# One encoder layer on one core: first loads and first norm by blocks of tokens, and a reordered preparation of the pairs of heads

## The reference, cut to what matters

```python
hn = rms_norm(h, norm_mix)
proj = hn @ w_in                      # 2048 x 5248
u_r, q, k, v = split(proj)
u_r = u_r + mu_prev * (prev - u_r) + mu_next * (next - u_r)   # first 3712 columns
y_r = rwkv7_bidirectional(u_r, ...)   # 16 heads of 64: LoRA terms, a state of 64x64 per head and direction
y_a = rms_norm(window_attention(q, k, v, sink, bias))
h = h + concat([y_r, y_a]) @ w_out
h = h + memory_cross_attention(rms_norm(h), rms_norm(mem))
h = h + hierarchical_moe(rms_norm(h))
return rms_norm(h, final_norm)
```

## Time and profile before

| | before |
|---|---|
| median of 3 runs | 1913.31 us (1912.08 to 1913.46) |
| the profiled execution's own time | 1915.28 us |
| its span, first to last instruction | 1913.5 us |
| busy: PE, DVE, ACT, POOL | 88%, 23%, 16%, 4% |
| mean granted TensorE clock | 0.964 |

### The profile page before, as it was taken

The page is one execution under the profiler, slowest core; times in us unless marked ns, Lnnn a source line. Parts: engine busy times, 40 slices in busy tenths (PEclk is TensorE's granted clock), DMA queues, the critical chain, the costliest instruction groups (busy, mean ns, idle before and its releaser), DMA issues.

```text
span 1913.5 us, 36816 instructions
## 1 busy us (share of the span) xinstructions
PE 1676.4 (88%) x16304; PEld 1194.8 (62%) x16304; DVE 447.1 (23%) x1018; ACT 313.7 (16%) x806; POOL 86.0 (4%) x143
## 2 busy tenths in 40 slices
PE   3999999978788899999899798888988889888884
PEld 2888888867667644766777456555565555655552
DVE  1100333477776410112311011110111101111014
ACT  2112222155556300113100000000000000000001
POOL 1000000000000000002000000000000000000000
PEclk9999999999888999999899999999999999999997
DMA  9734333500000274332399999999999999999995
GB/s 312 129 67 156 125 113 131 213 20 3 4 3 4 84 270 176 133 154 95 143 426 421 428 430 418 425 435 418 431 422 426 434 415 430 421 412 433 425 434 240
DMA packets 95221, 509.75 MB, mean 266 GB/s; under 512 B 39308, under 2 KB 43808, under 8 KB 77072
## 3 DMA queue, kind: packets, MB, share of 16 engines
q1 hardware_dynamic: 86376, 487.65, 63.0%
q0 software_dynamic: 7808, 17.28, 2.9%
q10 hardware_dynamic: 936, 3.28, 0.6%
HBM read 497.66 MB, written 23.10 MB: 272 GB/s over the span
## 4 chain that ended last, share of the span: by engine, by line
PE 68%; DMA 20%; DVE 6%; issue 2%; ACT 2%; SPq 1%; DVEq 0%; POOL 0%; ACTq 0%
PE ps L1887 18%; DMA ring<-in_wu 18%; PE ps L1385 14%; PE ps L1710 6%; PE ps L1875 6%; PE ps L1937 6%; PE ps L1728 1%; PE ps L1779 1%; PE ps L1737 1%; SPq L271 1%; PE ps L1796 1%; PE ps L1538 1%; PE ps L1467 1%; PE ps L1426 1%; PE ps L1448 1%
## 5 line engine op out<-in xcount | busy, mean ns | idle before, releaser
L1887 PE MATMUL ps<-ring,rkv 128*64 128x256 f32 x4096 | 469.4, 390 | 69.8 <-DMA ring<-in_wu 46.8
L1887 PEld LDWEIGHTS ps<-ring,rkv 128*64 128x64 f32 x4096 | 333.1, 140 | 214.2 <-DMA ring<-in_wu 56.1
L1385 PE MATMUL ps<-hnT,ring 128*128 128x256 f32 (+1 forms) x1280 | 282.2, 379 | 2.1 <-ACT hnT L468 0.9
L1385 PEld LDWEIGHTS ps<-hnT,ring 128*128 128x128 f32 (+1 forms) x1280 | 239.1, 187 | 47.6 <-issue 10.1
L1937 PE MATMUL ps<-ring,gg 128*64 128x512 f32 x1024 | 236.5, 615 | 32.3 <-DMA ring<-in_wd 16.2
L1937 PEld LDWEIGHTS ps<-ring,gg 128*64 128x64 f32 x1024 | 83.7, 142 | 163.1 <-issue 143.9
L1301 DVE SCALAR_TENSOR_TENSOR gg<-ps,tmp,gg 128x256 f32<-128x256 f32 x32 | 15.5, 484 | 519.7 <-PE ps L1887 519.7
L1875 PE MATMUL ps<-hnT,sw 128*128 (+1 forms) x1024 | 122.7, 282 | 4.5 <-DVE hnT L1236 2.4
L1875 PEld LDWEIGHTS ps<-hnT,sw 128*128 128x128 f32 x1024 | 119.4, 197 | 10.6 <-issue 8.3
L727 ACT ACTIVATE rkv<-ps 128x512 f32<-128x512 f32 x32 | 19.1, 597 | 546.1 <-PE ps L1937 546.1
L1309 DVE COPY rkv<-ps 128x512 f32<-128x512 f32 x31 | 21.4, 692 | 242.7 <-PE ps L1937 242.7
(11 more groups left out here) (340 smaller groups left out, 1627.5 us busy)
## 6 DMA issues: line engine op xcount, KB each, us to landing
ring<-in_wg SPq DMA_DIRECT2D x32, 4096.0 KB, 19.8
ring<-in_wu SPq DMA_DIRECT2D x32, 4096.0 KB, 21.4
ring<-in_wd SPq DMA_DIRECT2D x32, 4096.0 KB, 18.1
ring<-in_w_in SPq DMA_DIRECT2D x7, 4096.0 KB, 15.1
ring<-in_w_out SPq DMA_DIRECT2D x4, 4096.0 KB, 22.5
ring<-in_w_in SPq DMA_DIRECT2D x16, 512.0 KB, 7.5
y_dram<-tmp POOLq DMA_DIRECT2D x1, 4096.0 KB, 21.7
ring<-in_xatt_wk SPq DMA_DIRECT2D x1, 4096.0 KB, 13.9
```

Of the source, the lines that this page charges most:

```text
L1385: ins = mm(ps[0:rows_, m % 2, 0:T], lhs, hnT[:, k, :], start=k == 0, stop=k == KD - 1)
L1887: ins = mm(ps[CAP * h:CAP * h + CAP, bank, 0:T], xT[:, k, CAP * i:CAP * i + CAP], slot_k(slot)[:, k, T * h:T * h + T], start=k == 0, stop= ...
```

## The change

1. `x` comes in two transfers of 128 tokens (`x_in0`, `x_in1`). SP's six parameter rows go out ahead of the weights n=0, and the three LoRA matrices move from ACT's queue to SP's, behind n=1 and ahead of n=2 (and ahead of SP's wait for `prm_tr`).
2. The first norm goes by blocks of 128 tokens: squares, square root, reciprocal, scaling and 16 transposes for one block, then the other. DVE's wait for the turned parameters stands between the blocks. The copies out still need both blocks.
3. ACT loads the square root table with a dummy activation on `warm` right behind its first issues, again at the start of each pair but the last, and the exponential table behind the copies of the solutions.
4. `quotients(p + 2)` moves ahead of DVE's wait for step 7; `products_ar(p + 1, 1)` behind the copy `Yp`.
5. ACT's exponentials 0 to 2 wait for DVE's first carried terms (`rw_tte`) and not for `rw_gnow`; number 3 moves behind the copies of states and keeps the wait for `rw_gnow`.

```diff
-            sp.dma_start(tokA[:], xv).then_inc(S["x_in"], 16)
+            for b in range(TB):
+                sp.dma_start(tokA[:, b], xv[:, b]).then_inc(S[f"x_in{b}"], 16)
+            rows(sp, 1)
...
-                if n == 1:
-                    rows(sp, 1)
                 if n == 2:
+                    sp.dma_start(dw2, ...); sp.dma_start(aw2, ...); sp.dma_start(gw2, ...)
                     sp.wait_ge(S["prm_tr"], 1)
...
             pool (first):
+            pool.memset(warm, 1.0)
...
             rows(act, 0)
-            act.dma_start(dw2, ...); act.dma_start(aw2, ...); act.dma_start(gw2, ...)
+            A(warm, warm, ACT.Sqrt)
...
-            squares(0, S["x_in"], 16)
-            std(0, 1)
+            for b in range(TB):
+                act.wait_ge(S[f"x_in{b}"], 16)
+                A(tokB[:, b, :], tokA[:, b, :], ACT.Square, accum_out=stat(0, 0)[:, b:b + 1]).then_inc(S["sq_done"], 1)
+                act.wait_ge(S["first_var"], b + 1)
+                A(stat(0, 2)[:, b:b + 1], stat(0, 1)[:, b:b + 1], ACT.Sqrt).then_inc(S["first_std"], 1)
...
             def exponential(p, n, now=False):
                 if n == 0:
                     act.wait_ge(S["rw_q"], p + 1)
-                    if not now:
-                        act.wait_ge(S["rw_gnow"], p)
+                if n == 3 and not now:
+                    act.wait_ge(S["rw_gnow"], p)
...
             ACT, pair_:
+                if not last:
+                    A(warm, warm, ACT.Sqrt)
                 for g in range(4):
                     act.wait_ge(S["rw_x0"], 4 * p + g + 1)
...
                 if next_:
-                    for n in range(4):
+                    A(warm, warm, ACT.Exp)
+                    act.wait_ge(S["rw_tte"], 4 * p + 1)
+                    for n in range(3):
                         exponential(p + 2, n)
...
                 if next_:
-                    for n in range(4, 8):
+                    for n in range(3, 8):
                         exponential(p + 2, n)
...
             DVE, first norm:
-            normed(0)
-            dve.wait_ge(S["prm_tr"], 1)
-            V.tensor_copy(prm[:, 0:208], ps[:, 7, 0:208]).then_inc(S["prm_ok"], 1)
+            for b in range(TB):
+                one = slice(b, b + 1)
+                dve.wait_ge(S["sq_done"], b + 1)
+                V.tensor_scalar(stat(0, 1)[:, one], ...).then_inc(S["first_var"], 1)
+                dve.wait_ge(S["first_std"], b + 1)
+                dc.link(V.reciprocal(stat(0, 2)[:, one], stat(0, 2)[:, one]))
+                V.tensor_scalar(tokB[:, b, :], tokA[:, b, :], ...).then_inc(S[("first_hn", "hn_done")[b]], 1)
+                if b == 0:
+                    dve.wait_ge(S["prm_tr"], 1)
+                    V.tensor_copy(prm[:, 0:208], ps[:, 7, 0:208]).then_inc(S["prm_ok"], 1)
...
             DVE, pair_:
+                if next_:
+                    quotients(p + 2)
                 dve.wait_ge(S["rw_pt"], 24 * p + 8)
                 if not first:
                     variance(ps[:, 7, T:2 * T])
                 V.tensor_copy(PRN[0][:, 3]...).then_inc(S["rw_pv"], 1)
-                if next_:
-                    quotients(p + 2)
...
                     V.tensor_copy(gam_now, gam).then_inc(S["rw_gnow"], 1)
-                    products_ar(p + 1, 1)
                 dve.wait_ge(S["rw_y0"], 2 * p + 2)
                 V.tensor_copy(Yp..., ps[:, 0:4, T:T + CH]).then_inc(S["rw_y0e"], 1)
                 if not last:
                     dve.wait_ge(S["rw_gnow"], p + 2)
+                    products_ar(p + 1, 1)
                     products_bk(p + 1, 1)
...
             PE, first turn:
-            pe.wait_ge(S["hn_done"], 1)
-            turn(0)
+            for b in range(TB):
+                pe.wait_ge(S[("first_hn", "hn_done")[b]], 1)
+                for k in range(KD):
+                    ins = tr(ps[:, k // 2, ...], tokB[:, b, P * k:P * k + P], ident)
```

More of the change, by code:

```diff
@@ L129, in encoder @@
         exps = sb("exps", [P, 32])
+        warm = sb("warm", [P, 1])[:]
         ps = ctx.enter_context(nc.psum_tensor("ps", [P, 8, 512], F32))
@@ L283, in _ @@
                     sp.wait_ge(used[s], uses[n] - 1)
-                if n == 1:
-                    rows(sp, 1)
                 if n == 2:
+                    sp.dma_start(dw2, a["decay_w2"].rearrange("z r c -> r z c")).then_inc(S["lora_in"], 16)
+                    sp.dma_start(aw2, a["iclr_a2"].rearrange("z r c -> r z c")).then_inc(S["lora_in"], 16)
+                    sp.dma_start(gw2, a["gate_w2"].rearrange("(k p) c -> p k c", p=P)).then_inc(S["lora_in"], 16)
                     sp.wait_ge(S["prm_tr"], 1)
@@ L567, in _ @@
                         exponential(0, n, now=True)
-                    std(4, 2)
+                    std(4, 1)
                 if j == 21:
@@ L623, in _ @@
             squares(1, S["mem_in"], 16)
-            std(1, 3)
+            std(1, 2)
             turned(1)
             squares(2, S["op_add"], 8)
-            std(2, 4)
+            std(2, 3)
             for f in range(4):
@@ L765, in normed @@
                 dve.wait_ge(S["sq_done"], 2 * n + 2)
-                rstd(n, D, EPS, n + 1 if n == 0 else n + 2)
+                rstd(n, D, EPS, n + 1)
                 for b in range(TB):
@@ L789, in turned @@
                     ins.then_inc(S["hn_ev_v"], 1)
-            normed(0)
-            dve.wait_ge(S["prm_tr"], 1)
-            V.tensor_copy(prm[:, 0:208], ps[:, 7, 0:208]).then_inc(S["prm_ok"], 1)
+            for b in range(TB):
+                one = slice(b, b + 1)
+                dve.wait_ge(S["sq_done"], b + 1)
+                V.tensor_scalar(stat(0, 1)[:, one], stat(0, 0)[:, one], 1.0 / D, EPS, ALU.mult, ALU.add).then_inc(S["first_var"], 1)
+                dve.wait_ge(S["first_std"], b + 1)
+                dc.link(V.reciprocal(stat(0, 2)[:, one], stat(0, 2)[:, one]))
+                V.tensor_scalar(tokB[:, b, :], tokA[:, b, :], stat(0, 2)[:, one], None, ALU.mult).then_inc(S[("first_hn", "hn_done")[b]], 1)
+                if b == 0:
+                    dve.wait_ge(S["prm_tr"], 1)
+                    V.tensor_copy(prm[:, 0:208], ps[:, 7, 0:208]).then_inc(S["prm_ok"], 1)
             dve.wait_ge(S["prm_ok"], 1)
@@ L1064, in _ @@
             dve.wait_ge(S["ya_sq"], 3)
-            rstd(4, C, EPS, 2)
+            rstd(4, C, EPS, 1)
             for b in range(TB):
@@ L1372, in _ @@
             pe.wait_ge(S["prm_ok"], 1)
-            pe.wait_ge(S["hn_done"], 1)
-            turn(0)
+            for b in range(TB):
+                pe.wait_ge(S[("first_hn", "hn_done")[b]], 1)
+                for k in range(KD):
+                    o = T * (k % 2) + P * b
+                    ins = tr(ps[:, k // 2, o:o + P], tokB[:, b, P * k:P * k + P], ident)
+                    if b and k % 2:
+                        ins.then_inc(S["hn_tr"], 1)
             pe.wait_ge(S["hn_ev_a"], 4)
```

15 lines of the change are left out of this document (6 added, 9 removed).

## The result

| | before | after |
|---|---|---|
| median of 4 runs each, same chip | 1912.69 us (1910.31 to 1913.46) | 1867.14 us (1865.04 to 1867.9) |
| the profiled execution's own time | 1915.28 us | 1867.9 us |
| its span | 1913.5 us | 1865.8 us |
| mean granted TensorE clock | 0.964 | 0.974 |

The change is faster: ratio 0.9762, interval 0.9745 to 0.9779. The gain is 45.6 us between the medians and 47.7 between the two spans, where 39.9 were forecast.

A forecast was written before the change was run, and what follows sets the result against it. TensorE carries 68% of the chain, so edits pay where it waits, at the start and in the pairs. 18.0 + 15.75 + 4.15 + 2 = 39.9 us from 1915.28 leaves 1875.4; less 1.97, 1873.4; range 1863 to 1884.

The forecast's parts named there:

- my sum: Whole kernel: the forecast's terms add up as priced, time 1868 to 1879 us; chance 0.58.
- the clock stays up: Rival for the pairs: TensorE's clock stays up in all of them, 8 us more than taken, time 1865; chance 0.09.
- The start, 18.0 forecast: Up to the first projection tile: 18.0 us won, between 18.8 (tokens decide) and 9.2 (n=0 at its old pace).
- So the weights decide: At the start: weights n=0, landing at 20.0, let go the first tile, as tokens would allow it at 19.2.
- Full pairs, 15.75 forecast: Pairs 1 to 5: 3.15 us won a pair through `quotients`, `products_ar` and ACT's earlier loads and exponentials, 15.75 in all.
- signs named ahead: Pairs: DVE idle at most 1.5 us before step 7, reciprocal behind root, L1667 not waiting for ACT, L1050 every 31 us.
- its bound of 3.9 a pair: Full pairs, upper bound: 2.54, 0.85 for ACT, and some 0.5 if TensorE takes the states sooner.
- The clock, 2 forecast: Pairs: shorter TensorE waits may keep the clock up in some, at most 10 us, against 4 lost; 2 us gain taken.
- Pairs 0, 6 and 7, 4.15 forecast: Remaining pairs: 2.2 us net in pair 0, 1.95 in pair 6, nothing in pair 7; together 4.15.
- n=0 at its old pace: Rival at the start: weights n=0 land at 28.8, gain there 9.2 us, time 1882; chance of n=0 late 0.14.
- Pairs at half their gain through another wait: Rival: TensorE's solutions or ACT's copies take over, 1.3 to 1.8 us a pair, time 1882; chance 0.13.
- The low clock moving into the Gram products: Rival, slower: low clock moves into Gram products and 24 steps, 8.7 us a pair, time 1934; chance 0.03.

The follow-up runs named there:

- lora_act: The changed kernel with the three LoRA matrices back on ACT's queue, behind its rows: 1879.86 us, ratio 0.9833.
- rows_back: The changed kernel with SP's six parameter rows back between the weights n=0 and n=1: 1876.14 us, ratio 0.9793.
- no_act: The changed kernel with the exponentials' order and waits as before and no dummy exponential: 1883.33 us, ratio 0.9836.
- better: The changed kernel with less DVE work between step 7 and `Yp`, the last gate product going to POOL: 1864.97 us, ratio 0.9742.
- no_ar: The changed kernel with `products_ar` back ahead of the copy `Yp`: 1873.31 us, ratio 0.9782.
- start_only: The changed kernel with the edits in the pairs undone: 1896.28 us, ratio 0.991.
- fill_before: The kernel before with 14 filler matmuls a pair into parts of PSUM that nothing reads: 1910.59 us, ratio 0.9986.
- no_quot: The changed kernel with `quotients` behind step 7 again: 1886.1 us, ratio 0.9849.
- no_loads: The changed kernel without the two dummy activations in the pairs: 1881.28 us, ratio 0.9832.
- pairs_only: The kernel before with only the pair edits (points 3 to 5), without the dummy root ahead of the first norm: 1884.1 us, ratio 0.9854.
- changed_again: The changed kernel itself once more, on the same chip as better: 1866.23 us, ratio 0.9755.
- no_quot_fill: The kernel no_quot with the 14 filler matmuls a pair of fill_before added: 1893.92 us, ratio 0.9883.

## Why the prediction was right or wrong

**Direction and places of the gains: right.** The start and the pairs both gave, as two sums that add up, and the stages behind passed the gain on. The size came near, but its terms missed both ways: less at the start, more in the pairs' order, the clock and pairs 6 and 7, and 1.1 lost behind the pairs. At 1867.14 the time lies just below the 1868 to 1879 of "my sum", and nearer the 1865 of the rival "the clock stays up", to which the prediction gave 0.09.

**The start, 18.0 forecast, 16.5 measured.** n=0 was sized well: forecast 20.0, landed 20.2, and lora_act and rows_back show both of the reasons given. The step that failed was "So the weights decide". Tokens were forecast ready at 19.2 and were at 21.56, for two reasons. The transposes of block 1 ended at 20.06 (13.80 + 6.26), not 18.3: they began at 13.80 and not at 13.1, and the 32 ran without a gap but took 6.26 us, 0.20 each, and not 5.17. With the same code for the start they took 4.93 us in no_act, 5.06 in better, 5.25 in no_ar and up to 6.46 in start_only, all at a granted clock of 1.00, so this part belongs to the execution; what sets it is open. And behind the last transpose I took 0.92 us from before, where the copies had begun early and had kept pace with the transposes (31.93 to 37.10):

```profile
33.16 0.88 DVE L788 TENSOR_SCALAR hnT<-ps,prm 128x256 f32<-128x256 f32 x2 [1.29 <-PE ps L1365]
```

Each copy needs both blocks; so now all 16, eight on DVE and eight on ACT, lie behind 18.01. They take 3.23 us there without a gap, and the tile follows the last of them. In the three kernels with short transposes the copies began 0.6 to 0.8 us earlier, and the tile came at 20.57 to 20.75: the copies decide, and not the 32 transposes' end.

**Full pairs, 15.75 forecast.** Measured are 25.8 in all, of which the clock is a part. In pair 3 (the rows' "pair 2"), which ran from 498.27 to 532.45 before and from 469.58 to 498.46 after, the gains are, stretch by stretch:

| step | forecast | measured |
|---|---|---|
| to step 7 (Gram products, 24 steps) | 0 | 12.05 to 11.64: 0.41 (clock) |
| step 7 to the reciprocal | 1.86 | 3.99 to 1.92: 2.07 |
| reciprocal to L1033 | 0 | 9.81 to 9.82: 0 |
| L1033 to the copy `Yp` | 0.68 | 2.88 to 2.12: 0.76 |
| `Yp` to the chain of states | 0.61 | 2.04 to 1.06: 0.98 |
| the chain to the end of the pair | 0 | 3.41 to 2.32: 1.09 (clock) |

Without the two rows of the clock, whose work did not change, the order gave 3.81, as fill_before says by another way (3.78). Of the three terms only the last was much mis-sized: I let the chain begin 1.44 us behind `Yp`, and it began at 1.06. In no_quot's pair 5, where the chain waits for nothing either but the clock is low, it began 1.31 behind (572.71 to 574.02); so 0.25 of the 0.38 is the full clock, which counts here only because ACT's wait is gone: in fill_before, at the full clock but with ACT's wait, it is 2.05 as before. Of the signs named ahead, the wait for step 7 (1.12, under 1.5), the reciprocal behind the root and the chain without a wait for ACT came as said; the pair's length, 28.9 and not 31, did not. 3.8 × 5 = 19.0, 3.3 above the forecast and inside its bound of 3.9 a pair.

The remark on ACT's table loads held: the dummy activation starts 1.30 us after its load (470.39 to 471.69), and ACT stands for nothing more. The Trainium skill, ScalarE: Activation LUTs, section What ACT_TABLE_LOAD costs, adds 1.38 us of drain to each switch. By it, one switch back on the path costs 2.66 us. no_loads puts one back, the root's, and lost 1.42 at the full clock, with the activation 1.29 us behind the start of its load (552.69 to 553.98). The measurement decides, for this load at this place.

**The clock, 2 forecast.** This is the largest error, and the term that was mis-sized. The rival "the clock stays up in all pairs" came true. 1.38 to 1.50 us a pair is 6.9 to 7.5 in pairs 1 to 5, some 5 above the 2 taken. I had its size within reach (1.7 a pair from the chain) and gave it away by taking "some" pairs and setting a loss against it. Pair 7 also gained 1.4 with no edit of its own that the forecast priced; its clock went from 0.96 to 1.00, and in start_only, without the pairs' edits, it gained 1.3 the same way. The Trainium skill, TensorE: Matmul & The Clock Gate, section HAM oscillation, says that idle times between bursts of matmuls bring the low clock back each time; that agrees with 0.89 in start_only, where the waits are the old ones, and 1.00 in pairs_only and fill_before, where they are shortened or filled. One of rows_back's pairs, with the shortened waits, still fell to 0.94.

**Pairs 0, 6 and 7, 4.15 forecast, 6.6 measured.** From the first tile to the end of pair 0 it gave 2.2, as forecast, but that stretch holds the projections too and gave 1.0 in changed_again (21.41 to 412.83); so this agreement may be luck. Pair 6 gave 2.97 instead of 1.95, and 3.93 in changed_again (28.90), so it varies by a microsecond between executions; why is open. Pair 7 gave 1.4 instead of nothing.

The sum closes, since its terms are stretches of the same two traces: 39.9 - 1.5 (start) + 3.3 (order) + 4.8 (clock in pairs 1 to 5) + 2.4 (pairs 6 and 7) = 48.9, less the 1.1 lost net behind pair 7: 47.8, against 47.7.

**The rivals that did not come.** n=0 at its old pace: excluded by lora_act, which brings it back by returning the LoRA traffic. Pairs at half their gain through another wait: not in the change, but it is what met better, one step further. The low clock moving into the Gram products: the opposite happened. Of the signs named for the start, the rows were there by 13 (12.67), but the first tile was let go by the tokens' copy and not by n=0.

## What to carry to other kernels

At a start that waits for several transfers, ask of each what it shares its bandwidth with and what stands ahead of it in its queue: here two moves had to be made together, and either alone left 7.5 to 8 us of the gain behind. Where an engine works without a gap between two waits of TensorE, look in its order for work that nothing needs yet, and move it into the wait ahead: 3.8 us a pair came from order alone. Price the clock for each repetition apart and for all of them: in no_loads two pairs with the same work ran at 1.00 and at 0.91, and an edit judged alone carries that with it. Matmuls that only fill time hold the clock, but look at TensorE's timeline for what they push back: they were free in fill_before and cost 1.39 us a pair in no_quot_fill.

## What the runs showed of the hardware

- The granted clock held at 1.00 through all full pairs of the changed kernel in both of its traces, though TensorE still waits in them (0.34 us for DVE at 494.99, for one); in rows_back, with the same pairs, one of the five fell to 0.94 and took 29.61 us. With an edit in the pairs taken back it fell in all five (no_quot, 0.86 to 0.92), in some (no_loads, 0.89 to 1.00) or in one (no_ar, 0.94).
- 14 idle matmuls a pair held it as well, for a gain of 1.38 us a pair in fill_before; in pair 7 they cost 2.6 us (30.42 against 27.78 in start_only, both at 1.00).
- An issue on SP's queue behind a large transfer stood 19.83 us in the kernel before and 9.29 us in rows_back, both times behind x and n=0; the same issue behind x alone took 0.42.
- 2.6 MB of LoRA matrices in flight took the core from 373 to 236 GB/s (24 to 34 us); from 34 us on it moved 385 again.
- A DVE instruction of 128x256 (L1048 of better) took 0.80 us beside a multiplication on POOL and 0.26 where POOL stood idle.
- 32 transposes of the same code at a granted clock of 1.00 took 4.93 to 6.46 us in different runs.
- A square root began 1.29 us after the start of its table load of 1.28; no further time showed between the two.
